# One fused encoder layer on one core: exponentials of the longest causal rows in two column pieces

## The chip, the cores and the metric

The kernel runs on one NeuronCore of one Trainium2 chip. The metric is device microseconds of that core, from the first to the last instruction and what lies around them; less is better. TensorE is called PE here (PEld is its loading of weights, which overlaps its matmuls), VectorE DVE, ScalarE ACT, GpSimd POOL, and SyncE SP.

## What is computed

One layer of a streaming encoder: 2048 prompt frames and 8 running streams of 16 frames, width 1024. RMSNorm, one projection to queries, keys, values and forget gates, two groups of 8 attention heads of 64, an output projection, and a SwiGLU block of width 2816. The change touches the first attention group only, on the prompt:

```
logf = log_sigmoid(f + b_forget);  C = cumsum(logf)            # per head
s    = q @ k.T * 64**-0.5 + (C[t] - C[s]);  s = -inf where key > query
p    = softmax(s, axis=-1);  out = p @ v                       # "fox": causal, 8 heads, 2048 x 2048
```

The second group ("band") sees its own chunk of 64 and the eight before it, with a learned bias; the streams attend to their caches.

## The kernel before

Three blocks follow each other: `front` (projection), `attend` (all attention), `output_and_ffn`. The change is inside `attend` (L658), from about 620 to 1283 us of the span.

Work comes as **jobs** (`all_jobs`, L569). A causal job ("fox", p, i) is one pair of heads p (0 to 3) and one block of 128 queries i (0 to 15); it has i + 1 key tiles of 128, so rows of 128 x 128 to 128 x 2048 for each of two heads e. There are 64 causal jobs, then 64 band jobs (at most 5 tiles) with 16 stream jobs between them. The tiles of a job are cut into **groups** of at most four (`job_groups`): jobs with i = 12 to 15 have four groups, those with i = 8 to 11 three.

For each job and group the engines do this:

- PE `score` (L1052): three high/low products of queries and keys into the PSUM tile `S[e]`, 128 x up to 512.
- DVE `biased` (L1313, L1348): adds the bias, writes the negated scores to `sx` in SBUF and keeps the running minimum in `nm`.
- ACT `exps` (L1198, L1214): once per job and head e, over the whole row, in place in `sx`, with the row's sum written by `accum_out` into `sums`. It waits until the job's last `biased` of that head, as it needs the minimum of the whole row. ACT shows such an instruction as an ACTIVATE and an ACTIVATION_READ_ACCUMULATOR behind it; `s_ex` counts them.
- PE `turn` (L1092, L1109): transposes the group's tiles into `pt[0]` (queries 0 to 63) and `pt[1]` (64 to 127); first all tiles of head 0, then all of head 1.
- ACT `copy` (L1217, L1225) copies `pt[0]` and DVE `copy` (L1351, L1359) copies `pt[1]` to `pts`. There is one `pt` pair, so `turn` of a group waits for both copies of the group before.
- PE `values` (L1129, L1147): `pts` times the values into `po`; DVE `evict` (L1378) takes `po` to `os_`, and SP stores it.

The order is a fixed list (`attend_order`, L625): the scores of job n + 2 are spread over the turns of job n. `value_order` (L641) says before which turns PE does `values` of groups that it holds back: for a job of four groups that is before its turns 1 and 3, for one of three groups before turns 0 and 1 of itself or of the next. A turn with `values` behind it is called long here, the others short. In the jobs of this change turns 0 and 2 are long, turns 1 and 3 short. `exps_after` (L683) puts the exponentials of job n + 1 behind ACT's copies of turns 0 (e = 0) and 2 (e = 1) of job n: only into long turns.

In `turn(n, 0)` PE waits for the exponential of head 0 ahead of its first transpose and for that of head 1 ahead of the transposes of head 1 (L1103). Each engine works through its list in order.

After the last job `turn_sums` (L1157) transposes all of `sums`, and DVE inverts it.

Of the kernel before, what the change touches and what calls it, by code (L numbers as in the profile page):

```python
# [7 lines left out]
ALU = mybir.AluOpType  # L8
ACT = mybir.ActivationFunctionType
# [4 lines left out]
P = 128  # L14
# [548 lines left out]
QB = SEQ // P  # L563
NPAIR = 2 * H // 2
# [16 lines left out]
JOBS = all_jobs()  # L581
NJOB = len(JOBS)
# [4 lines left out]
def is_stream(n):  # L587
    return JOBS[n][0] == "stream"
# [25 lines left out]
    return stream_keys(JOBS[n][1]) // 4 + 1 if is_stream(n) else len(job_groups(n))  # L614


def counted(sizes):

    out = [0]
    for s in sizes:  # L620
        out.append(out[-1] + s)
    return out
# [35 lines left out]
def attend(nc, t, keep, neg_c, recips):  # L658

    T0 = counted(len(job_groups(n)) for n in range(NJOB))  # L660
    S0 = counted(score_count(n) for n in range(NJOB))
    E0 = counted(1 if is_stream(n) else 2 for n in range(NJOB))
    M0 = counted(min(len(job_groups(n)[-1]), 2) for n in range(NJOB) if JOBS[n][0] == "fox")
    ORDER = attend_order()
    VALUES = value_order(ORDER)
# [17 lines left out]
    def exps_after(n):  # L683

        if not LONGS[n]:
            return 0, len(job_groups(n)) - 1
        return LONGS[n][0], LONGS[n][1 if len(LONGS[n]) > 1 else 0]

    with ExitStack() as ctx:
# [11 lines left out]
        pts = [m.sb(f"pts{u}", [P, 2, 4, P]) for u in range(NPT)]  # L701
        ot = m.sb("ot", [P, P])
        sums = m.sb("sums", [P, QB, 2, KD])
        stream_sums = [m.sb(f"stream_sums{u}", [P, 1]) for u in range(2)]
        os_ = [m.sb(f"os{u}", [P, P]) for u in range(NOS)]
        nm = [m.sb(f"nm{u}", [P, 2]) for u in range(NSX)]
# [27 lines left out]
        s_b0 = m.sem("bias_first")  # L734
        s_v0 = m.sem("v_first")
        s_os = [m.sem(f"o_stored{u}") for u in range(NOS)]
        (s_pool, s_mk, s_hi, s_lo, s_sc, s_bi, s_ex, s_tr, s_ca, s_cd, s_pv, s_ot, s_to, s_rc, s_ev, s_es, s_st, s_rd, s_far, s_near, s_brel) = (
            m.sem(n) for n in (
                "pool_consts", "masked_bias", "split_high", "split_low", "scores", "biased", "exp", "turned", "copied_act",
                "copied_dve", "pv", "stream_o", "stream_turned", "recips", "evicted", "stream_evicted", "sums_turned", "recips_stored", "far_in", "near_in", "tables"))  # L740
        l_k = [m.sem(f"cache_k{u}") for u in range(2)]
        l_v = [m.sem(f"cache_v{u}") for u in range(2)]
        l_b = [m.sem(f"cache_bias{u}") for u in range(2)]
# [51 lines left out]
        with nc.Block() as block:  # L795
# [236 lines left out]
            def _(pe):  # L1032
# [59 lines left out]
                def turn(n, g):  # L1092
                    G = T0[n] + g
                    tiles = job_groups(n)[g]
                    t0 = job_tiles(n)[0]
                    if G >= 1:
                        copied(G - 1)
                    if is_stream(n):
                        stream_turn(n, g)
                        return  # L1100
                    for e in range(2):
                        if g == 0:
                            pe.wait_ge(s_ex, E0[n] + e + 1)  # L1103
                        for j, kt in enumerate(tiles):
                            c = (kt - t0) * P
                            for x in range(2):
                                r = slice(64 * x, 64 * x + 64)
                                to = (4 * e + j) * 64
                                last = nc.tensor.transpose(pt[x][:, to:to + 64], sx[n % NSX][r, e, c:c + P], eye[r, r])  # L1109
                    last.then_inc(s_tr, 1)  # L1110
# [45 lines left out]

                def turn_sums():  # L1157
                    pe.wait_ge(s_ex, E0[NJOB])
                    pe.wait_ge(s_bi, 2 * S0[NJOB])
                    for u in range(2):  # L1160
                        last = nc.tensor.transpose(S[0][0][:, u * P:(u + 1) * P],
                                                   sums[:, u * QB // 2:(u + 1) * QB // 2].rearrange("p i e k -> p (i e k)"), eye[:])
                    last.then_inc(s_st, 1)
# [22 lines left out]
            @block.scalar  # L1186
            def _(act):
                def split_high(x):
                    p, c = x // 8, CHUNKS[x % 8]
                    u = p % 2  # L1190
                    cs = slice((c % 4) * 512, (c % 4 + 1) * 512)
                    act.wait_ge(s_raw[x % NRAW], 16 * (x // NRAW + 1))
                    if c < 4:
                        nc.scalar.activation(kh[u][:, cs], raw[x % NRAW][:], ACT.Copy).then_inc(s_hi, 1)
                    else:
                        nc.scalar.activation(qh[u][:, cs], raw[x % NRAW][:], ACT.Copy, scale=SCALE).then_inc(s_hi, 1)

                def exps(n, e):  # L1198
                    if is_stream(n):
                        if e == 1:  # L1200
                            return
                        act.wait_ge(s_bi, 2 * S0[n + 1])
                        w = stream_keys(JOBS[n][1]) * P + NQ
                    else:
                        act.wait_ge(s_bi, 2 * (S0[n + 1] - 1) + e + 1)
                        w = len(job_tiles(n)) * P
                    kind, p, i = JOBS[n]
                    if kind == "stream":
                        if p >= 2:
                            act.wait_ge(s_iv, p - 1)  # L1210
                        total = stream_sums[p % 2][:]
                    else:
                        total = sums[:, i, e, p:p + 1]
                    nc.scalar.activation(sx[n % NSX][:, e, :w], sx[n % NSX][:, e, :w], ACT.Exp, bias=nm[n % NSX][:, e:e + 1],  # L1214
                                         scale=-1.0, accum_out=total).then_inc(s_ex, 1)

                def copy(n, g, x):  # L1217
                    G = T0[n] + g
                    if by_dve(x):
                        return  # L1220
                    k = slot_count(n, g)
                    act.wait_ge(s_tr, G + 1)
                    if G >= NPT:
                        act.wait_ge(s_pv, G - NPT + 1)
                    nc.scalar.activation(pts[G % NPT][:, :, 0:k, 64 * x:64 * x + 64],  # L1225
                                         pt[x][:].rearrange("p (e j q) -> p e j q", e=2, q=64)[:, :, 0:k, :], ACT.Copy).then_inc(s_ca, 1)

                for x in range(2):
                    split_high(x)
                for e in range(2):  # L1230
                    exps(0, e)
                for what, n, g in ORDER:
                    if what == "turn":
                        more = n + 1 < NJOB
                        for x in range(2):
                            copy(n, g, x)
                        for e in range(2):
                            if more and g == exps_after(n)[e]:
                                exps(n + 1, e)
                        if last_of(n, g):  # L1240
                            for x in first_splits(n):
                                split_high(x)

            @block.vector
            def _(dve):
# [29 lines left out]
                def stream_pad():  # L1275
                    dve.wait_ge(s_tr, T0[WIDE])
                    nc.vector.memset(vnew, 0.0)
                    for u in range(2):
                        nc.vector.memset(qb[u], 0.0)
                    dve.drain().then_inc(s_pad, 1)  # L1280
                    dve.wait_ge(s_pad, 1)
# [106 lines left out]
                for what, n, g in ORDER:  # L1388
                    if what == "score":
                        biased(n, g)  # L1390
                    else:
                        if VALUES[n, g]:
                            for x in ended:
                                evict(x)
                            ended = []
                            for x in VALUES[n, g]:
                                if last_of(*x) and is_stream(x[0]):
                                    stream_outward(x[0])
                                    ended.append(x[0])
                                elif last_of(*x):  # L1400
                                    evict(x[0])
                        if n + 2 == STREAM_AT[0] and g == 0:
                            block_queries(0)
                        if n + 3 in STREAM_AT[1:] and g == 0:
                            block_queries(JOBS[n + 3][1])
                        copy(n, g)
                        for y in first_splits(n):
                            split_low(y)
                        if (n, g) == (6, 0):
                            stream_consts()  # L1410
                        if n == WIDE and g == 0:
                            stream_pad()
                invert_sums()
                for x in ended:
                    evict(x)
# [1255 lines left out]
```

## Time and profile before

| | us |
|---|---|
| median of 3 runs | 3012.16 |
| lowest, highest | 3006.19, 3015.57 |
| the profiled execution: time, span | 3007.07, 3005.3 |

| engine | busy us | share of the span |
|---|---|---|
| PE (matmul) | 2845.9 | 95% |
| PEld (weight load) | 2552.1 | 85% |
| DVE | 1709.5 | 57% |
| ACT | 1139.9 | 38% |
| POOL | 754.4 | 25% |

The granted clock of TensorE was 0.983 of full speed over the span. The rows below are read so: a timeline row is start, duration, engine, line, operation, what it writes and reads, its shape, how many instructions were merged, and in brackets how long the engine sat idle before it and whose end released it. "issue" means that no release is seen.

### The profile page before, as it was taken

The numbers are of one execution on the slowest core, as the hardware profiler recorded it, in microseconds if no ns is written. First come the engines' busy times: TensorE is split into PE (matmuls) and PEld (weight loads), VectorE is DVE, ScalarE is ACT, GpSimd is POOL, SyncE is SP. The second block draws the span as 40 slices with busy tenths as digits, with TensorE's granted clock in tenths as the row PEclk, the third lists the DMA queues.
The fourth block names the chain that finished last, engine by engine and source line by source line (L and its number), as shares of the span: only waits on it lengthen the run. The fifth ranks groups of instructions, "written<-read, shape, count | busy, mean of one in ns | idle before, by whom it ended". The sixth has DMA issues, their size and how long they took to land.

```text
span 3005.3 us, 54881 instructions
## 1 busy us (share of the span) xinstructions
PE 2845.9 (95%) x22143; PEld 2552.1 (85%) x22143; DVE 1709.5 (57%) x3122; ACT 1139.9 (38%) x1904; POOL 754.4 (25%) x683
## 2 busy tenths in 40 slices
PE   7999999979999789969989999999999999999998
PEld 7999999957777567758879999999999997887887
DVE  6222121168788577857788667776766662224443
ACT  5330000046666456645553334333433342223221
POOL 0000000054445123023345434544344420000000
PEclk9999999979999999989999999999999999999999
DMA  5322212152112897467733332332232345335553
GB/s 170 97 71 80 73 62 76 48 168 77 54 49 57 267 297 235 149 203 219 239 111 139 101 108 95 135 114 95 96 113 97 129 140 146 97 96 161 166 167 121
DMA packets 285539, 384.75 MB, mean 128 GB/s; under 512 B 24472, under 2 KB 211112, under 8 KB 273512
## 3 DMA queue, kind: packets, MB, share of 16 engines
q1 hardware_dynamic: 284984, 379.68, 40.0%
q8 instruction: 177, 2.90, 0.4%
q10 hardware_dynamic: 304, 1.57, 0.2%
q14 instruction: 74, 0.61, 0.1%
HBM read 291.91 MB, written 89.28 MB: 127 GB/s over the span
## 4 chain that ended last, share of the span: by engine, by line
PE 44%; issue 6%; DVE 3%; POOL 2%; DMA 1%; ACT 1%; SPq 0%; POOLq 0%; DVEq 0%; ACTq 0%
PE ffn_w L2174 3%; PE ffn_x L2174 3%; PE ffn_w L2177 3%; PE ffn_x L2177 3%; PE ffn_w L2176 3%; PE ffn_x L2176 3%; PE ffn_z L2177 3%; PE ffn_z L2174 3%; PE ffn_z L2176 3%; PE ffn_z L2208 1%; PE ffn_w L2208 1%; PE ffn_y L2174 1%; PE ffn_w L2210 1%; PE ffn_z L2210 1%; PE ffn_y L2177 1%
## 5 line engine op out<-in xcount | busy, mean ns | idle before, releaser
L1214 ACT ACTIVATE att_sx<-att_sx,att_nm 128x640 f32<-128x640 f32 (+17 forms) x272 | 263.4, 971 | 7.4 <-DVE att_nm L1348 7.4
L1225 ACT ACTIVATE att_pts<-att_pt 128x384 f32<-128x384 f32 (+3 forms) x296 | 145.3, 491 | 251.3 <-PE att_pt L1109 236.6
L80 PE MATMUL frt_pz<-frt_xhi,frt_hi 128*128 128x448 f32 (+1 forms) x640 | 230.5, 360 | 0.0
L82 PE MATMUL frt_pz<-frt_xhi,frt_lo 128*128 128x448 f32 (+1 forms) x640 | 230.5, 360 | 0.0
L81 PE MATMUL frt_pz<-frt_xlo,frt_hi 128*128 128x448 f32 (+1 forms) x640 | 230.0, 359 | 0.0
L1109 PEld LDWEIGHTS att_pt<-att_eye,att_sx 64*128 64x128 f32 x3296 | 129.9, 140 | 115.7 <-ACT att_pts L1225 60.1
L515 DVE TENSOR_TENSOR frt_shared<-frt_pz,frt_rb 128x448 f32<-128x448 f32 (+1 forms) x80 | 48.9, 612 | 313.5 <-PE frt_pz L82 313.5
L1109 PE MATMUL att_pt<-att_eye,att_sx 64*128 64x64 f32 x3296 | 166.5, 232 | 55.2 <-ACT att_pts L1225 18.3
L1147 PE MATMUL att_po<-att_pts,att_vv 128*64 128x128 f32 x3296 | 217.2, 279 | 0.3 <-issue 0.3
L1147 PEld LDWEIGHTS att_po<-att_pts,att_vv 128*64 128x64 f32 x3296 | 177.8, 137 | 45.1 <-ACT att_pts L1225 22.7
L1359 DVE COPY att_pts<-att_pt 128x384 f32<-128x384 f32 (+3 forms) x296 | 164.3, 555 | 64.6 <-PE att_pt L1109 58.4
L80 PE MATMUL frt_pv<-frt_hi,frt_xhi 128*128 128x256 f32 (+1 forms) x544 | 157.3, 289 | 18.5 <-DVE frt_lo L447 15.7
L2174 PE MATMUL ffn_z<-ffn_hh,ffn_wh 128*128 128x362 f32 (+1 forms) x528 | 173.2, 328 | 0.4 <-DVE ffn_hl L2413 0.4
L2177 PE MATMUL ffn_z<-ffn_hh,ffn_wl 128*128 128x362 f32 (+1 forms) x528 | 173.1, 328 | 0.0
L2176 PE MATMUL ffn_z<-ffn_hl,ffn_wh 128*128 128x362 f32 (+1 forms) x528 | 172.3, 326 | 0.0
L81 PE MATMUL frt_pv<-frt_lo,frt_xhi 128*128 128x256 f32 (+1 forms) x544 | 154.3, 284 | 0.0
L82 PE MATMUL frt_pv<-frt_hi,frt_xlo 128*128 128x256 f32 (+1 forms) x544 | 154.0, 283 | 0.0
L2396 DVE TENSOR_TENSOR ffn_wl<-ffn_tr,ffn_wh 128x2048 fp32r<-128x2048 f32 x66 | 152.3, 2308 | 0.4 <-ACT ffn_wh L2239 0.4
L371 ACT ACTIVATE frt_hi<-frt_raw,frt_gain 128x256 fp32r<-128x256 f32 x96 | 41.4, 497 | 270.6 <-DMA frt_raw<-in_w_slab 270.6
L2424 DVE TENSOR_TENSOR ffn_al<-ahead_first,ffn_ah 128x2816 fp32r<-128x2816 f32 x32 | 99.0, 3093 | 75.9 <-ACT ffn_ah L2281 74.6
L2139 POOL TENSOR_TENSOR ffn_rr<-ffn_vv,ffn_power 128x1 f32<-128x1 f32 x17 | 9.4, 550 | 498.8 <-DVE ffn_vv L2444 498.8
L2239 ACT ACTIVATE ffn_wh<-ffn_tr 128x2048 fp32r<-128x2048 f32 x66 | 126.1, 1911 | 14.9 <-POOL ffn_tr L2094 14.9
(327 smaller groups left out, 8300.6 us busy)
## 6 DMA issues: line engine op xcount, KB each, us to landing
ahead_first<-mid_act SPq DMA_DIRECT2D x68, 704.0 KB, 6.7
ahead_second<-in_w_gu SPq DMA_DIRECT2D x33, 1024.0 KB, 5.4
ffn_wr<-in_w_gu SPq DMA_DIRECT2D x33, 1024.0 KB, 5.3
att_raw<-out_zT SPq DMA_DIRECT2D x64, 256.0 KB, 4.7
att_bb<-in_cache_ak SPq DMA_DIRECT2D x16, 1024.0 KB, 10.4
att_bb<-in_cache_av SPq DMA_DIRECT2D x16, 1024.0 KB, 8.3
mid_act<-ffn_ao SPq DMA_DIRECT2D x44, 362.0 KB, 2.5
out_zT<-frt_shared SPq DMA_DIRECT2D x64, 224.0 KB, 1.9
```

The lines of the kernel that those rows point to most:

```text
L80: nc.tensor.matmul(out, a_hi(k), b_hi(k), start=(k == 0), stop=False)
L81: nc.tensor.matmul(out, a_hi(k), b_lo(k), start=False, stop=False)
L82: last = nc.tensor.matmul(out, a_lo(k), b_hi(k), start=False, stop=(k == kk - 1))
L1109: last = nc.tensor.transpose(pt[x][:, to:to + 64], sx[n % NSX][r, e, c:c + P], eye[r, r])
L1147: last = nc.tensor.matmul(po[n % 2][r, 0:P], vv[u][:, kt, r], pts[G % NPT][:, e, j, :], start=(g == 0 and j == 0), stop=(g == len(groups) ...
L1214: nc.scalar.activation(sx[n % NSX][:, e, :w], sx[n % NSX][:, e, :w], ACT.Exp, bias=nm[n % NSX][:, e:e + 1], scale=-1.0, accum_out=total).t ...
L1225: nc.scalar.activation(pts[G % NPT][:, :, 0:k, 64 * x:64 * x + 64], pt[x][:].rearrange("p (e j q) -> p e j q", e=2, q=64)[:, :, 0:k, :], A ...
L1359: nc.vector.tensor_copy(pts[G % NPT][:, :, 0:k, 64:128], pt[1][:].rearrange("p (e j q) -> p e j q", e=2, q=64)[:, :, 0:k, :]).then_inc(s_c ...
L2174: nc.tensor.matmul(out, high[:, k, :], hh[x][:, k, :w], start=(k == 0 and not more), stop=False, skip_group_check=True)
L2176: nc.tensor.matmul(out, high[:, k, :], hl[x][:, k, :w], start=False, stop=False, skip_group_check=True)
L2177: last = nc.tensor.matmul(out, low[:, k, :], hh[x][:, k, :w], start=False, stop=end, skip_group_check=True)
L2396: nc.vector.tensor_tensor(wl[n % 2][:, 1:], tr[:], f32(wh[n % 2][:, 1:]), ALU.subtract).then_inc(lt, 1)
```

## The change

Causal jobs with i >= 11 (twelve key tiles or more: five jobs of each pair, 20 in all) get each head's exponential in two column pieces, cut at a whole tile: 6 + 6, 6 + 7, 7 + 7, 7 + 8 and 8 + 8 tiles for i = 11 to 15. The four pieces x = 0 to 3 (head 0 left, head 0 right, head 1 left, head 1 right) stand behind ACT's copy of turn min(x, last) of the job before. Behind a job of four groups (i = 12, 13, 14) that is one piece per turn, 0 to 3; behind one of three groups (i = 10, 11) pieces 2 and 3 both stand behind turn 2. The sums of the right pieces go to a new tile `more_sums`, which DVE adds to `sums` once, in job 72; `turn_sums` waits for that. PE's waits count two pieces for a head.

```
+LONG_ROW = 11
+def row_pieces(n):
+    return 2 if JOBS[n][0] == "fox" and JOBS[n][2] >= LONG_ROW else 1
-    E0 = counted(1 if is_stream(n) else 2 for n in range(NJOB))
+    E0 = counted(1 if is_stream(n) else 2 * row_pieces(n) for n in range(NJOB))
+        more_sums = m.sb("more_sums", [P, QB - LONG_ROW, 2, NPAIR // 2])
...
 def turn(n, g):   # PE
-                            pe.wait_ge(s_ex, E0[n] + e + 1)
+                            pe.wait_ge(s_ex, E0[n] + row_pieces(n) * (e + 1))
...
 def turn_sums():   # PE
+                    pe.wait_ge(s_ms, 1)
...
+                def exps_long(n, x):   # ACT
+                    kind, p, i = JOBS[n]
+                    e, h = divmod(x, 2)
+                    act.wait_ge(s_bi, 2 * (S0[n + 1] - 1) + e + 1)
+                    w = len(job_tiles(n)) * P
+                    cut = w // 2 // P * P
+                    cs = slice(cut, w) if h else slice(0, cut)
+                    total = more_sums[:, i - LONG_ROW, e, p:p + 1] if h else sums[:, i, e, p:p + 1]
+                    nc.scalar.activation(sx[n % NSX][:, e, cs], sx[n % NSX][:, e, cs], ACT.Exp, bias=nm[n % NSX][:, e:e + 1],
+                                         scale=-1.0, accum_out=total).then_inc(s_ex, 1)
...
-                        for e in range(2):
-                            if more and g == exps_after(n)[e]:
-                                exps(n + 1, e)
+                        if more and row_pieces(n + 1) == 2:
+                            for x in range(4):
+                                if g == min(x, len(job_groups(n)) - 1):
+                                    exps_long(n + 1, x)
+                        elif more:
+                            for e in range(2):
+                                if g == exps_after(n)[e]:
+                                    exps(n + 1, e)
...
+                        if n == WIDE + 8 and g == 0:   # DVE
+                            dve.wait_ge(s_ex, E0[WIDE])
+                            joined = sums[:, LONG_ROW:, :, 0:NPAIR // 2]
+                            nc.vector.tensor_tensor(joined, joined, more_sums[:], ALU.add).then_inc(s_ms, 1)
```

## Rows read from the trace of the kernel before

**Rows 1.** Page, part 1: busy time, share and instructions of each engine.
```profile
PE 2845.9 (95%) x22143; PEld 2552.1 (85%) x22143; DVE 1709.5 (57%) x3122; ACT 1139.9 (38%) x1904; POOL 754.4 (25%) x683
```
**Rows 2.** Busy time by stretch: two causal stretches, band and streams; then clock, DMA.
```profile
620.00:811.50 191.50, 171.44 (x2624) 135.47 (x2624) 153.26 (x456) 121.83 (x218) 96.17 (x122) 0.95 0.28 88
811.50:990.50 179.00, 167.72 (x2656) 133.45 (x2656) 146.76 (x433) 117.73 (x208) 81.95 (x97) 1.00 0.23 73
990.50:1283.00 292.50, 256.72 (x4326) 194.12 (x4326) 216.87 (x798) 167.34 (x418) 65.20 (x68) 0.97 0.76 236
```
**Rows 3.** Page, part 5: exponentials; loads of the transposes (busy, mean ns, idle before).
```profile
L1214 ACT ACTIVATE att_sx<-att_sx,att_nm 128x640 f32<-128x640 f32 (+17 forms) x272 | 263.4, 971 | 7.4 <-DVE att_nm L1348 7.4
...
L1109 PEld LDWEIGHTS att_pt<-att_eye,att_sx 64*128 64x128 f32 x3296 | 129.9, 140 | 115.7 <-ACT att_pts L1225 60.1
```
**Rows 4.** Waits from 763 to 811.5 us, rows 11 to 15 of pair 1.
```profile
PEld att_pt L1109 <- ACT att_pts L1225: 6.2, 9, 1.0
```
**Rows 5.** Timeline around turn 0 of jobs i = 13, 14, 15 of pair 1.
```profile
785.14 0.60 ACT L1225 ACTIVATE att_pts<-att_pt 128x512 f32<-128x512 f32 x1 [0.60 <-PE att_pt L1109]
...
785.90 0.48 PEld L1109 LDWEIGHTS att_pt<-att_eye,att_sx 64*128 64x128 f32 x12 [0.48 <-ACT att_pts L1225]
...
787.24 0.55 DVE L1359 COPY att_pts<-att_pt 128x384 f32<-128x384 f32 x1
...
794.18 0.60 ACT L1225 ACTIVATE att_pts<-att_pt 128x512 f32<-128x512 f32 x1 [0.73 <-PE att_pt L1109]
...
794.94 0.48 PEld L1109 LDWEIGHTS att_pt<-att_eye,att_sx 64*128 64x128 f32 x12 [0.49 <-ACT att_pts L1225]
...
802.18 0.69 DVE L1359 COPY att_pts<-att_pt 128x512 f32<-128x512 f32 x1 [1.63 <-PE att_pt L1109]
...
802.33 0.59 ACT L1225 ACTIVATE att_pts<-att_pt 128x512 f32<-128x512 f32 x1
...
802.97 0.58 PEld L1109 LDWEIGHTS att_pt<-att_eye,att_sx 64*128 64x128 f32 x16 [0.98 <-ACT att_pts L1225]
```
**Rows 6.** Timeline of ACT: exponentials of 896 and 1024 columns.
```profile
736.33 1.03 ACT L1214 ACTIVATE att_sx<-att_sx,att_nm 128x896 f32<-128x896 f32 x1
737.26 0.19 ACT L1214 ACTIVATION_READ_ACCUMULATOR att_sx<-att_sx,att_nm 128x1 f32 x1
737.35 1.03 ACT L1214 ACTIVATE att_sx<-att_sx,att_nm 128x896 f32<-128x896 f32 x1
...
740.31 1.14 ACT L1214 ACTIVATE att_sx<-att_sx,att_nm 128x1024 f32<-128x1024 f32 x1
741.35 0.19 ACT L1214 ACTIVATION_READ_ACCUMULATOR att_sx<-att_sx,att_nm 128x1 f32 x1
```
**Rows 7.** Timeline: PE released by the end of an exponential.
```profile
620.78 0.19 ACT L1214 ACTIVATION_READ_ACCUMULATOR att_sx<-att_sx,att_nm 128x1 f32 x1
...
621.02 0.18 PEld L1109 LDWEIGHTS att_pt<-att_eye,att_sx 64*128 64x128 f32 x2 [4.88 <-ACT att_sx L1214]
```
**Rows 8.** Timeline: exponentials in jobs of three groups, and the turns behind them.
```profile
767.89 0.60 ACT L1225 ACTIVATE att_pts<-att_pt 128x512 f32<-128x512 f32 x1 [1.03 <-PE att_pt L1109]
768.38 1.57 ACT L1214 ACTIVATE att_sx<-att_sx,att_nm 128x1536 f32<-128x1536 f32 x1
...
770.21 0.58 PEld L1109 LDWEIGHTS att_pt<-att_eye,att_sx 64*128 64x128 f32 x16 [0.17 <-issue]
...
776.15 1.67 ACT L1214 ACTIVATE att_sx<-att_sx,att_nm 128x1664 f32<-128x1664 f32 x1
...
778.20 0.45 PEld L1109 LDWEIGHTS att_pt<-att_eye,att_sx 64*128 64x128 f32 x12 [0.17 <-issue]
```
**Rows 9.** DVE: evictions in the attention block as a group.
```profile
L1378 DVE COPY att_os<-att_po 128x128 f32<-128x128 f32 x127 | 36.7, 289 | 35.1 <-PE att_po L1147 26.7 <-DMA mid_mixT<-att_os 7.5
```
**Rows 10.** Timeline of DVE in job 72, where the joining of the sums is put.
```profile
1032.43 0.29 DVE L1378 COPY att_os<-att_po 128x128 f32<-128x128 f32 x1 [2.73 <-DMA mid_mixT<-att_os]
```
**Rows 11.** Busy time by stretch, right after the wait of Rows 10.
```profile
1032.90:1036.00 3.10, 2.98 (x46) 2.67 (x50) 2.28 (x11) 2.00 (x5) 2.95 (x3) 0.50 0.99 370
```

More of the change, by code:

```diff
@@ L736, in attend @@
         s_os = [m.sem(f"o_stored{u}") for u in range(NOS)]
-        (s_pool, s_mk, s_hi, s_lo, s_sc, s_bi, s_ex, s_tr, s_ca, s_cd, s_pv, s_ot, s_to, s_rc, s_ev, s_es, s_st, s_rd, s_far, s_near, s_brel) = (
+        (s_pool, s_mk, s_hi, s_lo, s_sc, s_bi, s_ex, s_tr, s_ca, s_cd, s_pv, s_ot, s_to, s_rc, s_ev, s_es, s_st, s_rd, s_ms, s_far, s_near, s_brel) = (
             m.sem(n) for n in (
                 "pool_consts", "masked_bias", "split_high", "split_low", "scores", "biased", "exp", "turned", "copied_act",
-                "copied_dve", "pv", "stream_o", "stream_turned", "recips", "evicted", "stream_evicted", "sums_turned", "recips_stored", "far_in", "near_in", "tables"))
+                "copied_dve", "pv", "stream_o", "stream_turned", "recips", "evicted", "stream_evicted", "sums_turned", "recips_stored", "sums_joined", "far_in", "near_in", "tables"))
         l_k = [m.sem(f"cache_k{u}") for u in range(2)]
```

## The prediction

> **What bounds the kernel now.** I read the page's busy table first, then the busy time by stretch, then the waits of the causal rows, and last the timeline of three job boundaries. The page says that PE is busy for 95% of the span [rows 1]. The stretches say the same for the part that the change touches: PE is busy for 167.72 of 179.00 us from 811.5 to 990.5 (pairs 2 and 3), while ACT has 117.73 us of work there [rows 2]. So PE sets the time, ACT has about a third of its time free, and an exponential matters only where PE waits for it. The 272 exponentials with their accumulator reads take 263.4 us of ACT [rows 3]; the question is where PE stands still for them.
>
> In rows 11 to 15 of a pair it does not. The largest wait of the loads for transposes there is for ACT's copies of `pt` (6.2 us in nine places), and a wait for an exponential does not occur among the rows of that view [rows 4]. These nine are the short turns: PE turns a group, has little else to do, and needs the copies before it may turn the next. At the boundary from i = 12 to i = 13 the copy of turn 3 starts at 785.14, and PE starts turn 0 of the next job at 785.90 after 0.48 us idle; the same at 794.18 and 794.94, and at 802.33 and 802.97 (0.98 us idle there, for no score lies between) [rows 5]. ACT has no exponential in these short turns; it does all of them in the long ones, where PE has `values` to do meanwhile: from the start of a copy to PE's next turn it is 0.76 us in a short turn (785.14 to 785.90) and 2.32 us in a long one (767.89 to 770.21) [rows 5, 8].
>
> **What the change removes.** The 40 exponentials of 1536 to 2048 columns in long turns become 80 of half the length. Where did the long ones make anybody late? One place shows: ahead of turn 3 of i = 14, DVE copies at 802.18 and ACT only at 802.33, with no idle time in front, since its exponential of 2048 columns had just ended [rows 5]. That is 0.15 us, four times in the kernel: at most 0.6 us to be gained. Elsewhere ACT is idle for 0.60 and 0.73 us ahead of such copies [rows 5], so nothing is released by shortening what comes before.
>
> The Trainium skill has a rule for this change: Perfetto Trace Analysis, section Optimizing Scalar/DVE Operations, says that where ScalarE is not saturated but causes bubbles on other engines, breaking up its instructions may let work finish sooner. Its first condition holds here; the second does not in the trace, as the waits of these rows name no exponential. By the rule alone the 0.6 us above would be the whole effect.
>
> **What it adds on ACT.** Per split, one fixed part and one accumulator read. An exponential of 896 columns starts the next instruction 1.02 us later (736.33 to 737.35): the read starts after 0.93, lasts 0.19, and overlaps the next by 0.10. For 1024 columns the read starts after 1.04 (740.31 to 741.35) [rows 6]. A piece of 768 is then 0.91 us (0.11 less than 896), and two take 1.82 us before the next instruction starts, against 1.56 for the whole 1536 (1.57 less the same 0.01) [rows 8]: 0.26 us a split, 10 us of ACT time over 40. ACT has it to spare; alone it costs nothing. What matters is where the last piece lands.
>
> **The new wait.** Behind jobs with four groups (i = 12, 13, 14), piece 3 stands behind the copy of turn 3. That is a short turn, and PE's next work but the score is turn 0 of the next job, whose second half (head 1) needs piece 3. The wait is worked out three times, each from the start of ACT's copy of turn 3:
>
> - the copy holds ACT for 0.49 us (767.89 to 768.38) [rows 8];
> - the piece: 0.93 + 0.19 = 1.12 us to the end of its read for 896 columns, 1.04 + 0.19 = 1.23 for 1024 [rows 6];
> - PE's first load follows the end of the read by 0.05 us (620.78 + 0.19 = 620.97 to 621.02) [rows 7].
>
> In the kernel before, the first load for head 1 begins in the middle of the burst. A load lasts 0.14 us [rows 3], so twelve in 0.48 us start (0.48 - 0.14) / 11 = 0.031 apart and the seventh comes 0.185 us after the first; of sixteen in 0.58 the ninth comes 0.235 after it [rows 5].
>
> - i = 12 to 13 (14 tiles, piece of 896): 785.14 + 0.49 + 1.12 + 0.05 = 786.80, against 785.90 + 0.185 = 786.08: 0.72 us later.
> - i = 13 to 14 (15 tiles, piece of 1024): 794.18 + 0.49 + 1.23 + 0.05 = 795.95, against 794.94 + 0.185 = 795.13: 0.82 us.
> - i = 14 to 15 (16 tiles, piece of 1024): ACT's copy now starts with DVE's at 802.18, so 802.18 + 1.77 = 803.95, against 802.97 + 0.235 = 803.21: 0.74 us. The 0.15 us gained above is in this.
>
> Sum 2.28 us a pair, four pairs: 9.1 us. Behind the waiting transposes stand the rest of turn 0, the score of n + 3, the held `values` and turn 1; all of them are PE's own and run without a gap, so none of it is caught up. DVE can't give it back either: its copy of turn 0 of i = 13 already started as late as 787.24, behind its own work [rows 5], so it is hardly moved, but PE needs that copy only after `values`. The later waits of PE are for copies that follow its own turns and move with it.
>
> **Pieces that cost nothing.** Pieces 0 and 2 lie in long turns, where whole rows fitted. Piece 1 lies behind turn 1, which is short: it makes ACT's copy of turn 2 late by up to some 0.2 us, but PE needs that copy only for its next turn, 2.32 us after the copy's start by the row above, and the copy takes 0.60. `values` is the cover; if it were gone, 12 x 0.2 = 2.4 us. Behind jobs of three groups (i = 10, 11) pieces 2 and 3 follow each other behind turn 2, which is long. For i = 11: 768.38 + 0.91 + 0.82 + 0.19 + 0.05 = 770.35 (the read 0.82 into a piece of 768, by the 0.11 us between 896 and 1024), needed by the ninth load at 770.21 + 0.235 = 770.45; for i = 12: 776.15 + 0.91 + 0.93 + 0.19 + 0.05 = 778.23, needed at 778.20 + (0.45 - 0.14) / 11 x 6 = 778.37 [rows 6, 8]. They fit, with 0.10 and 0.14 us to spare; I take 0, and 0.3 us each (2.4 us over eight) as the upper end.
>
> The joining of the sums is one DVE instruction on 128 x 40 elements. No row of before shows its shape; the nearest is a copy of 128 x 128 at 0.289 us [rows 9], so between 0 and 0.29, and I take 0: in job 72 DVE stands idle for 2.73 us soon after that place, until a store has landed [rows 10]. Without that cover it costs its 0.29 once. The waits that it adds are for things long done.
>
> **The sum.** +9.1 us, all of it one new wait of PE at 12 places. The profiled execution took 3007.07 us with a span of 3005.3, so its like would be 3016.2; the median of the runs is 5.1 us above it, and I forecast from the median: 3012.16 + 9.1 = 3021.3, with 3016 to 3026 as this case's own range, for the three runs lie 9.4 us apart.
>
> **The rivals.**
>
> A second bound on ACT (slower still): the margins of 0.10 and 0.14 us behind i = 10 and 11 are not there, or the late copies of turn 2 are waited for. It adds 2.4 us: 3023.7. For it: the margins are small. Against: the same pitches give both sides. Chance 0.10.
>
> The wait falls into slack (not slower): from 990.5 on, DMA is busy for 0.76 of the time and PE for 256.72 of 292.50 us [rows 2], and DVE waited 7.5 us for stores there [rows 9]. If those transfers ran on a clock of their own, a PE that comes 9.1 us later would find them done and wait less. It decides once the loads of that stage start irrespective of PE; then the 9.1 us vanish and the 0.6 us remain: 3011.6. Against: SP issues the first cache loads and queries behind waits for PE's and DVE's last causal jobs, so they move along. Chance 0.12.
>
> The clock falls: right after PE had stood still beside DVE's 2.73 us, its granted clock was 0.50 for a stretch of 3.10 us [rows 10, 11], the lower level of 1.2 GHz. If each of the 12 new stalls did this, about half of 3.10 us would be lost each time: 12 x 1.55 = 18.6 us more, 3039.9. Against: stalls of 0.98 us are there already [rows 5], and the stretch from 811.5 to 990.5 that holds them has 1.00 [rows 2]. The Trainium skill, TensorE: Matmul & The Clock Gate, section Part 1, gives the rule that too little recent work of PE halves its clock; the trace agrees that short stalls are no such case. Chance 0.04.
>
> **How the numbers follow.** Forecast 0.74, second bound 0.10, slack 0.12, clock 0.04. About 0.3% (9.0 us) is what a measurement of this kernel can tell from no change, and the forecast lies just on that line, at 9.1: half of its chance on either side. Slower: 0.37 + 0.10 + 0.04 = 0.51. Within: 0.37 + 0.08 = 0.45. Faster, from slack of more than was asked for: 0.04. The range for 8 in 10 goes from 3011, which takes in part of the slack case, to 3028.
>
> **What would show it.** In the changed kernel: 232 + 80 = 312 exponentials; in short turn 3 of i = 12, 13 and 14 an ACTIVATE of 896 or 1024 columns behind the copy; in turn 0 behind it PE's loads broken in two bursts of 6 or 8, the second released by ACT's exponential, about 0.7 to 0.8 us of new idle time, 12 times, 9 us in the waits under that name; the stretch of rows 12 to 15 of each pair 2.3 us longer, and all after 990.5 merely shifted; granted clock 1.00 in the causal rows. The forecast is wrong if that wait is there and the stretch from 990.5 to the end grows shorter, if the second burst starts sooner than 0.05 us behind the read, or if the rows i = 11 and 12 show broken bursts too.

## The result, and the profile after

The changed kernel takes 3021.07 us (median of 10 runs, 3018.23 to 3027.76) against 3012.73 us of the kernel before (10 runs, 3006.19 to 3017.14). The ratio is 1.0031, 95% interval 1.0020 to 1.0042: slower by 0.3%. The forecast was 3021.3.

The profiled execution has a span of 3018.6 us. First the busy table of the changed kernel, part 1 of its page, which answers to [rows 1]:

```profile
PE 2851.1 (94%) x22143; PEld 2555.4 (85%) x22143; DVE 1707.0 (57%) x3123; ACT 1149.6 (38%) x1984; POOL 753.8 (25%) x683
```

PE has the same 22143 matmuls. ACT has 80 instructions more (40 pieces, each with its read) and 9.7 us more of busy time; DVE has one more. The span grew by 13.3 us. PE's busy time grew by 5.2 with no matmul more; 2.3 of them lie in the causal rows (295.87 to 298.13 us over the stretch measured below), where a burst in two halves is counted as 0.40 + 0.40 us against 0.59 in one. The rest is waiting. Where it is shows in the waits of the loads for transposes, from 660 to 1005 us of the changed kernel (waiting instruction, releaser: us in total, times, longest):

```profile
PEld att_pt L1117 <- ACT att_pts L1245: 38.4, 61, 1.0
...
PEld att_pt L1117 <- ACT att_sx L1215: 8.0, 12, 0.7
PEld att_pt L1117 <- ACT att_sx L1234: 2.1, 9, 0.3
```

L1215 is the exponential in pieces, L1234 the whole one. In the kernel before, the same stretch has 38.5 us in 61 places for the copies and 2.1 us in nine for exponentials, all in short rows. So one line is new: 12 waits, 8.0 us, all for a piece. The timeline of the changed kernel around turn 0 of i = 13 in pair 1, the place of the first lines of [rows 5]:

```profile
789.13 0.60 ACT L1245 ACTIVATE att_pts<-att_pt 128x512 f32<-128x512 f32 x1 [1.28 <-PE att_pt L1117]
...
789.62 1.03 ACT L1215 ACTIVATE att_sx<-att_sx,att_nm 128x896 f32<-128x896 f32 x1
...
789.89 0.29 PEld L1117 LDWEIGHTS att_pt<-att_eye,att_sx 64*128 64x128 f32 x6 [0.49 <-ACT att_pts L1245]
...
790.56 0.19 ACT L1215 ACTIVATION_READ_ACCUMULATOR att_sx<-att_sx,att_nm 128x1 f32 x1
...
790.80 0.26 PEld L1117 LDWEIGHTS att_pt<-att_eye,att_sx 64*128 64x128 f32 x6 [0.61 <-ACT att_sx L1215]
...
791.88 0.74 PEld L1155 LDWEIGHTS att_po<-att_pts,att_vv 128*64 128x64 f32 x14 [0.36 <-ACT att_pts L1245]
```

The burst of twelve loads is in two halves. The first comes 0.76 us after the start of the copy, as before. The second waits until 790.80, which is 0.05 us behind the end of the read (790.56 + 0.19). Then PE goes on with its scores. The same for i = 14 and for i = 15, each one timeline of the changed kernel:

```profile
799.62 0.29 PEld L1117 LDWEIGHTS att_pt<-att_eye,att_sx 64*128 64x128 f32 x6 [0.49 <-ACT att_pts L1245]
...
800.63 0.26 PEld L1117 LDWEIGHTS att_pt<-att_eye,att_sx 64*128 64x128 f32 x6 [0.72 <-ACT att_sx L1215]
```

```profile
807.65 0.69 DVE L1384 COPY att_pts<-att_pt 128x512 f32<-128x512 f32 x1 [1.64 <-PE att_pt L1117]
807.65 0.60 ACT L1245 ACTIVATE att_pts<-att_pt 128x512 f32<-128x512 f32 x1 [0.58 <-PE att_pt L1117]
...
808.41 0.36 PEld L1117 LDWEIGHTS att_pt<-att_eye,att_sx 64*128 64x128 f32 x8 [0.94 <-ACT att_pts L1245]
...
809.42 0.32 PEld L1117 LDWEIGHTS att_pt<-att_eye,att_sx 64*128 64x128 f32 x8 [0.66 <-ACT att_sx L1215]
```

In the last one ACT's copy starts together with DVE's, and no longer 0.15 us behind it. For the first half of the burst that is worth only 0.03 us: it comes 0.76 us after the start of DVE's copy, where it came 0.79 us after it before (802.18 to 802.97 in [rows 5]), since PE needs DVE's copy as well, and that takes 0.69 us. The second half hangs on ACT's piece and has the whole 0.15, in front of a larger wait.

The same places in all four pairs can be compared by the first load of each turn. From turn 0 of job 10 (673.35 us before, 675.22 after) to turn 0 of job 64, the first band job (990.55 and 1001.07), it is 317.20 us before and 325.85 after: 8.65 us longer. Between turn 0 and turn 1 of rows 13, 14 and 15 the shift grows by 0.69, 0.79 and 0.76 us in each pair, 8.97 in all, and from any other turn to the next it changes by at most 0.03. The other 4.65 us of the 13.3 lie outside: 1.87 before job 10, and 2.78 behind job 64. Stages there vary by as much from profile to profile (below). The medians differ by 8.3 us, and the interval of the ratio goes from 6 to 13 us.

The joined sums, and what follows them on DVE in the changed kernel:

```profile
1040.27 0.19 DVE L1441 TENSOR_TENSOR att_sums<-att_sums,att_more_sums 128x40 f32<-128x40 f32 x1
...
1042.55 0.29 DVE L1403 COPY att_os<-att_po 128x128 f32<-128x128 f32 x1 [1.41 <-DMA mid_mixT<-att_os]
```

0.19 us, and 1.41 us of idle time behind it, as in [rows 10].

### The profile page after: what moved, and what is told of

Same layout as the page of the kernel before. It is cut to its first block, busy times and chain, and to the rows that moved or that the text cites. A ratio compares the mean times of both kernels' runs of the same rounds, so it can differ in the third digit from the quotient of the medians.

```text
span 3018.6 us, 54962 instructions
## 1 busy us (share of the span) xinstructions
PE 2851.1 (94%) x22143; PEld 2555.4 (85%) x22143; DVE 1707.0 (57%) x3123; ACT 1149.6 (38%) x1984; POOL 753.8 (25%) x683
## 3 DMA queue, kind: packets, MB, share of 16 engines
q10 hardware_dynamic: 304, 1.57, 0.2%
## 4 chain that ended last, share of the span: by engine, by line
PE 44%; issue 6%; DVE 3%; POOL 2%; DMA 1%; ACT 1%; SPq 0%; POOLq 0%; DVEq 0%; ACTq 0%
PE ffn_w L2203 3%; PE ffn_w L2206 3%; PE ffn_x L2203 3%; PE ffn_w L2205 3%; PE ffn_x L2206 3%; PE ffn_x L2205 3%; PE ffn_z L2206 3%; PE ffn_z L2203 3%; PE ffn_z L2205 3%; PE ffn_z L2237 1%; PE ffn_z L2239 1%; PE ffn_w L2237 1%; PE ffn_y L2203 1%; PE ffn_w L2239 1%; PE ffn_z L2238 1%
## 5 line engine op out<-in xcount | busy, mean ns | idle before, releaser
L1234 ACT ACTIVATE att_sx<-att_sx,att_nm 128x640 f32<-128x640 f32 (+12 forms) x232 | 192.0, 831 | 7.3 <-DVE att_nm L1373 7.3
```

## The experiments

Two theories. **A**: the loss is PE's wait for the piece in the short turn 3, and nothing else. **B**: the loss comes with the split itself, from more ACT instructions or their overlap with PE, wherever they stand. Each edit is against the changed kernel unless it is said otherwise. "Stretch" is the time from turn 0 of job 10 to turn 0 of job 64 in the one profile of each kernel, with the same rule as above; the ratio is that of the runs to those of the kernel before on the same chip (median 3012.87 for e1 to e4, 3013.04 for e5 and e6), and not quite the quotient of the medians. There are 11 runs of each experiment, but five of e3 and of e5. The stretch is the sharper of the two measures for this question.

| kernel | median us | ratio (95%) | stretch us | against before |
|---|---|---|---|---|
| before | 3012.73 | | 317.20 | |
| changed | 3021.07 | 1.0031 (1.0020 to 1.0042) | 325.85 | +8.65 |
| e1 wait for left pieces | 3009.57 | 0.9996 (0.9986 to 1.0006) | 316.99 | -0.21 |
| e2 split, old places | 3010.93 | 0.9995 (0.9986 to 1.0004) | 318.66 | +1.46 |
| e3 whole row behind turn 3 | 3034.24 | 1.0082 (1.0068 to 1.0096) | 341.86 | +24.66 |
| e4 last piece 256 columns | 3013.10 | 1.0003 (0.9994 to 1.0011) | 318.61 | +1.41 |
| e5 last piece 1536 columns | 3029.51 | 1.0056 (1.0044 to 1.0069) | 334.71 | +17.51 |
| e6 rows 11 and 12 alone | 3010.73 | 0.9991 (0.9982 to 1.0000) | 317.03 | -0.17 |

### e1: the same pieces, waited for only where they are read

Turn 0 reads at most four tiles, and every left piece has six or more.

```
-                        if g == 0:
-                            pe.wait_ge(s_ex, E0[n] + row_pieces(n) * (e + 1))
+                        if row_pieces(n) == 2:
+                            if g == 0:
+                                pe.wait_ge(s_ex, E0[n] + 2 * e + 1)
+                            elif g == 1 and e == 0:
+                                pe.wait_ge(s_ex, E0[n] + 4)
+                        elif g == 0:
+                            pe.wait_ge(s_ex, E0[n] + e + 1)
```

> The changed kernel with one difference: in turn 0 of a long row PE waits only for the left pieces (heads 0 and 1), and for the right pieces in turn 1, which is the first that can reach their tiles. ACT's list is the same. If the 8 to 9 us come from PE's wait for piece 3 (theory A), the 12 broken bursts are whole again, the causal stretch is as long as before within 0.6 us, and the time is that of before, 3012 to 3013. If they come from more ACT instructions or their overlap with PE, wherever they are waited for (theory B), about 8 us stay: 3020 to 3021.

Measured: 3009.57 us, ratio 0.9996; the stretch is 0.21 us shorter than before. The timeline of this kernel at the same place, turn 3 of i = 12 and turn 0 of i = 13:

```profile
786.35 0.60 ACT L1250 ACTIVATE att_pts<-att_pt 128x512 f32<-128x512 f32 x1 [1.28 <-PE att_pt L1122]
...
786.84 1.04 ACT L1220 ACTIVATE att_sx<-att_sx,att_nm 128x896 f32<-128x896 f32 x1
...
787.11 0.48 PEld L1122 LDWEIGHTS att_pt<-att_eye,att_sx 64*128 64x128 f32 x12 [0.49 <-ACT att_pts L1250]
...
787.77 0.19 ACT L1220 ACTIVATION_READ_ACCUMULATOR att_sx<-att_sx,att_nm 128x1 f32 x1
...
787.87 0.48 ACT L1250 ACTIVATE att_pts<-att_pt 128x384 f32<-128x384 f32 x1
```

The piece is where the change puts it, still runs while PE transposes, and ACT's next copy follows its read with no idle time; the burst is whole and the loss is gone. That is theory A, with everything of B left in place. Ahead of row 15 PE's turn comes 0.03 us sooner than before in each of the four pairs; this 0.12 us is all that splitting the long exponentials gives back to PE there. The change had asked PE to wait for columns that the turn does not read.

### e2: the same pieces in the places of the whole rows

```
-                                if g == min(x, len(job_groups(n)) - 1):
+                                if g == exps_after(n)[x // 2]:
```

> Rows split as in the change, but both pieces of a head stand where the whole row stood before: behind the long turns 0 and 2. Theory A (only the place in the short turn costs): no broken bursts, save that two pieces of 1024 hold ACT for 2.26 us against 1.99, so ahead of turn 3 of i = 14 ACT copies 0.27 us later: 4 x 0.27 = 1.1 us, 3013.8. Theory B (the split itself costs): 8 us, 3021.

Measured: 3010.93 us, ratio 0.9995; no wait for a piece among PE's waits, and a stretch 1.46 us longer than before where 1.1 were expected. Behind turn 2 of i = 14 (this kernel's timeline) two pieces hold ACT past the end of turn 3:

```profile
804.72 1.14 ACT L1215 ACTIVATE att_sx<-att_sx,att_nm 128x1024 f32<-128x1024 f32 x1
805.42 0.69 DVE L1384 COPY att_pts<-att_pt 128x512 f32<-128x512 f32 x1 [1.64 <-PE att_pt L1117]
805.76 0.19 ACT L1215 ACTIVATION_READ_ACCUMULATOR att_sx<-att_sx,att_nm 128x1 f32 x1
805.85 0.58 ACT L1245 ACTIVATE att_pts<-att_pt 128x512 f32<-128x512 f32 x1
806.48 0.58 PEld L1117 LDWEIGHTS att_pt<-att_eye,att_sx 64*128 64x128 f32 x16 [1.24 <-ACT att_pts L1245]
```

ACT copies 0.43 us behind DVE (0.15 before), and PE's idle time before its turn is 1.24 us where it was 0.98. A second place was missed in the expectation: ahead of turn 2 of i = 12 the idle time is 0.57 instead of 0.40, since ACT leaves its two pieces of 896 columns late. These two places make the shift grow by 0.27 and 0.17 us in each pair. Splitting costs some ACT time, and PE sees it only where ACT had none left.

### e3: no split, the whole row in the short turn

Against the kernel before:

```
     def exps_after(n):
+        if n + 1 < NJOB and JOBS[n + 1][0] == "fox" and len(job_groups(n)) == 4:
+            return LONGS[n][0], 3
```

> The kernel before, no split, but behind jobs i = 12, 13, 14 the whole exponential of head 1 stands behind turn 3 instead of turn 2. Theory A: the wait grows with the length of what stands there: 1792 columns give 785.14 + 0.49 + 1.68 + 0.19 + 0.05 - 786.08 = 1.47 us, 1920 give 1.57, 2048 give 1.60 (with ACT's 0.15 us of lateness gone), 4.64 a pair, 18.6 in all: 3031.3. Theory B: no added ACT instruction, so the time of before, 3012.7.

Measured: 3034.24 us, ratio 1.0082, stretch +24.66 us. Without any added instruction the kernel loses nearly three times what the change loses, so the place alone makes such a loss; that the split adds nothing to it is shown by e1. The waits of rows 13 and 14 cost 1.45 and 1.54 us, as worked out (1.47, 1.57), but row 15 costs 3.0 to 3.2 us where 1.60 was expected. Here is that place, first PE and ACT in the timeline:

```profile
812.10 0.35 PEld L1111 LDWEIGHTS att_pt<-att_eye,att_sx 64*128 64x128 f32 x8 [0.94 <-ACT att_pts L1227]
...
813.96 0.51 PEld L1111 LDWEIGHTS att_pt<-att_eye,att_sx 64*128 64x128 f32 x8 [1.51 <-ACT att_sx L1216]
...
815.33 2.63 PEld L1149 LDWEIGHTS att_po<-att_pts,att_vv 128*64 128x64 f32 x32 [0.22 <-ACT att_pts L1227]
```

and the stretches around it (busy time of PE, PEld, DVE, ACT, POOL, then the granted clock):

```profile
803.20:812.00 8.80, 6.11 (x116) 5.38 (x116) 4.08 (x13) 5.39 (x9) 1.07 (x3) 1.00 0.03 9
...
814.20:816.20 2.00, 2.00 (x22) 1.78 (x22) 1.45 (x5) 0.98 (x3) 0.00 (x0) 0.50 0.00 0
816.20:818.20 2.00, 2.00 (x30) 1.83 (x28) 0.02 (x2) 0.00 (x0) 0.00 (x0) 0.74 0.00 0
818.20:822.00 3.80, 2.92 (x63) 2.75 (x64) 1.68 (x3) 1.20 (x2) 0.00 (x0) 1.00 0.08 22
```

PE's loads stood idle for 0.94 us, went on for 0.35, and stood idle for 1.51; the granted clock then was 0.50, the lower level of 1.2 GHz, and a burst of 32 loads for `values` that lasts 1.73 us elsewhere took 2.63. That is the clock rival of the prediction, at a place where the stall is longer: 1.5 us each time, in all four pairs, 6 of the 24.66 us. The Trainium skill, TensorE: Matmul & The Clock Gate, section Part 1, says that the clock follows PE's recent activity; this trace agrees.

### e4 and e5: the size of the last piece

```
-                    cut = w // 2 // P * P
+                    cut = w - 2 * P if e else w // 2 // P * P                       # e4
+                    cut = max(w - 12 * P, w // 2 // P * P if w <= 13 * P else 0) if e else w // 2 // P * P   # e5
```

> The changed kernel with head 1 cut at w - 256 columns, so that the piece in the short turn 3 has 256 columns (0.40 us to its read and 0.19 of read). The number of ACT instructions is that of the change. Theory A: the wait shrinks to 0.19, 0.18 and 0.10 us for i = 13, 14, 15, 0.47 a pair, 1.9 us in all: 3014.6. Theory B: 8 us as in the change, 3021.

Measured e4: 3013.10 us, ratio 1.0003, stretch +1.41 us (1.9 expected; the shift grows by 0.15, 0.15 and 0.12 us in rows 13, 14 and 15 where 0.19, 0.18 and 0.10 were expected). With the same number of ACT instructions as the change, five sixths of the loss are gone.

> The changed kernel with head 1 of rows of 14, 15 and 16 tiles cut at w - 1536 columns: 1536 columns stand in the short turn 3 (a size between the change's 1024 and the 2048 that cost more than their length). By the end of the read alone (1.47 + 0.19 us after the start) the waits are 1.26, 1.25 and 1.17 us, 3.68 a pair, 14.7 in all: 3027.6. If PE's clock falls in row 15 as it did with 2048 columns (1.5 us there, four times), 20.7: 3033.6.

Measured e5: 3029.51 us, ratio 1.0056, stretch +17.51 us: between the two numbers given. The shift grows by 1.22, 1.22 and 1.19 us in rows 13, 14 and 15, which makes 14.5 in four pairs. In row 15 of pairs 1 and 3 it is 2.7 us instead, of pairs 0 and 2 it is not. The four places have the same waits (0.94, then 1.09 us) but not the same clock, and what decides between them was not found. These are the busy times by stretch of e5 from turn 0 to turn 1 of row 15, for pairs 0 to 3; the granted clock is the number behind POOL.

```profile
717.20:721.30 4.10, 3.13 (x54) 2.73 (x54) 1.37 (x5) 2.35 (x5) 0.55 (x1) 1.00 0.03 6
810.20:815.90 5.70, 4.67 (x54) 4.12 (x54) 1.37 (x5) 2.42 (x5) 0.62 (x2) 0.72 0.00 0
904.90:909.10 4.20, 3.17 (x56) 2.76 (x56) 1.38 (x5) 2.41 (x5) 0.61 (x2) 1.00 0.02 4
998.00:1003.70 5.70, 4.73 (x56) 4.15 (x56) 1.37 (x5) 2.35 (x5) 0.00 (x0) 0.72 0.53 198
```

From turn 0 to turn 1 of row 15 the granted clock is 0.72 or 0.73 in all four pairs of e3, and 1.00 in all four of the changed kernel.

So the loss against the size of the piece is 1.4 us at 256 columns, 8.65 at 896 and 1024, 14.5 at 1536 and 18.6 at 1792 to 2048 (24.66 less 6), with the clock on top at the two largest.

### e6: the change for rows 11 and 12 alone

```
-    return 2 if JOBS[n][0] == "fox" and JOBS[n][2] >= LONG_ROW else 1
+    return 2 if JOBS[n][0] == "fox" and JOBS[n][2] in (11, 12) else 1
```

The joining adds these two rows only.

> The change for rows i = 11 and 12 alone, those behind jobs of three groups; rows 13 to 15 are whole as before. Theory A: no piece stands in a short turn 3, margins of 0.10 and 0.14 us hold, no broken burst: the time of before, 3012.9. If the margins don't hold: up to 0.3 us eight times, 3015.3. Theory B (the split costs wherever it stands): 16 of 40 splits, about 3.3 us, 3016.

Measured: 3010.73 us, ratio 0.9991, stretch 0.17 us shorter than before. The narrow place ahead of row 11, which answers to the first rows of [rows 8], in the timeline of e6:

```profile
770.07 0.93 ACT L1215 ACTIVATE att_sx<-att_sx,att_nm 128x768 f32<-128x768 f32 x1
...
770.90 0.19 ACT L1215 ACTIVATION_READ_ACCUMULATOR att_sx<-att_sx,att_nm 128x1 f32 x1
770.98 0.58 PEld L1117 LDWEIGHTS att_pt<-att_eye,att_sx 64*128 64x128 f32 x16 [0.17 <-issue]
```

The read ends at 771.09, with 0.05 at 771.14, and the ninth load is due at 770.98 + 0.235 = 771.21. It fits by 0.07 us, and the burst is whole. Ahead of row 12 the same sum in e6 leaves 0.12 us.

No kernel here beats the one before: e1 and e6 are at its time within their intervals.

What lies outside the stretch moves by itself. The first transpose of the attention block starts between 620.97 and 623.42 us in the eight profiles, and from the last turn to the end it takes 1720.1 to 1723.7 us, in no order that follows the edits: e6, the fastest ratio, has the longest tail. From turn 0 of job 64 to the last turn it takes 291.1 to 294.5 us, and 298.9 in e5. Why these vary was not looked into.

## Why the prediction was right

- **What bounds.** PE, and ACT only where PE waits for it: 80 more ACT instructions cost PE nothing in e1.
- **The new wait.** Forecast 0.72, 0.82 and 0.74 us for rows 13, 14 and 15, together 9.1 us; measured 0.69, 0.79 and 0.76, together 8.97. The stretch grew by 8.65, as 0.12 us comes back ahead of row 15 and 0.20 in differences of 0.03 and less elsewhere. The parts of each sum (0.49 for the copy, 1.12 or 1.23 for the piece, 0.05 for the release) are in the trace after as they were before: 789.13 + 0.49 + 1.12 + 0.05 = 790.79, and PE loads at 790.80. That the medians came out within 0.3 us of the forecast (3021.07 against 3021.3) is in part luck, since their interval is some 6.6 us wide: the term is confirmed by the trace and not by the time.
- **Nothing catches up.** Confirmed: the shift stays in place to the end of the causal rows, and the medians differ by 8.3 us.
- **The pieces that cost nothing.** The rows behind jobs of three groups have no broken burst, by margins of 0.07 and 0.12 us in e6 against the 0.10 and 0.14 worked out. The late copies of turn 2 were not waited for: in e1, where the same pieces stand in front of them, the stretch is not longer.
- **The gain of 0.15 us** ahead of row 15 was rightly counted within the 0.74 for the second half of the burst, but it was mis-sized as a gain for PE by itself. The prediction left out that PE waits for DVE's copy too, so with the longer exponential out of the way PE's turn comes 0.03 us sooner and not 0.15: 0.12 us over four pairs in e1 where the prediction has at most 0.6. The sum did not rest on it; the rival of slack (3011.6) did.
- **Slack in the stream stage**, the rival of the other side: the stage behind job 64 took no less after the change (294.46 us to the last turn, 294.05 before). This stage varies by some 3 us between profiles, so alone it could not rule out a small part; that all of the 9.1 us were lost in slack is ruled out by the ratio, whose interval begins at 1.0020, or 6 us.
- **The clock rival** did not come about in the change, whose causal rows keep a granted clock of 1.00 from turn 0 of job 10 to turn 0 of job 64. Its price was right (1.55 us a place by [rows 11], 1.5 in e3), and the argument against it was too easy: that single stalls of 0.98 us are harmless says little of two with a short burst between. The change has 0.94 and 0.66 us at that place, e5 has 0.94 and 1.09, and there the clock fell in half of the cases.
- **The rule on breaking up instructions** (the Trainium skill, Perfetto Trace Analysis, section Optimizing Scalar/DVE Operations) asks for bubbles that the instructions cause. There were none here but 0.03 us in four places, and the split made new ones by where its last piece was put and how it was waited for. In e1 what the split gives is left alone: the stretch is 0.21 us shorter, below what the runs can tell.

What was not settled is on which side of 0.3% it would come out; it was called even, and the measured 0.31% is on the line as well.

## What to carry to other kernels

Before splitting an instruction, ask what its last piece releases, and how long the waiting engine has until it needs it: a piece half as long but one turn later is later by the turn. When an instruction is split, split the wait too; a consumer that still waits for the last piece gains nothing from the first. In this kernel that cured the loss (e1) but won nothing, for there was no wait to win back. And a transfer of work between turns is priced from the trace to some hundredths of a microsecond: end of the instruction in front, length of the piece, release, against the moment of first use.

## What the runs showed of the hardware

- An exponential of f32 in SBUF takes 1.03 us at 896 columns and 1.14 at 1024, whether it is a whole row or half of one, and 2.00 at 2048 (whole rows alone).
- PE's load starts 0.05 us behind the end of the accumulator's read that it waits for, at the places looked at (790.75 to 790.80, 800.58 to 800.63, 809.37 to 809.42, and 813.91 to 813.96 in e3).
- Behind two idle times of PE with a short burst between them the granted clock fell, to 0.50 where it was looked at closely: after 0.94 and 1.51 us in four of four places, after 0.94 and 1.09 in two of four, after 0.94 and 0.66 in none of four, read from turn 0 to turn 1 of row 15 in each pair. A single idle time of 1.24 us (e2) cost no such shift. The slow stretch behind cost 1.5 us each time.
